# Two of the three conv projections of a two-layer mixer moved to matmuls with 512 moving columns, in two alternating bank pairs

## What is computed

```
proj = h @ w_in
b_a, c_a, x_a, u_p, q, k, v, ga, gp, gt = jnp.split(proj, split_points(), axis=-1)
y_a = short_conv_mixer(b_a, c_a, x_a, conv_w, w_a_out)

def short_conv_mixer(b_gate, c_gate, xin, conv_w, w_out):
    u = c_gate * xin
    y = lax.conv_general_dilated(u, conv_w, ..., feature_group_count=u.shape[-1])
    return (b_gate * y) @ w_out
```

## Time and profile before

| | us |
|---|---|
| median of 3 runs | 1310.85 (1310.82 to 1310.9) |
| the profiled execution | 1310.87 |
| its span, first to last instruction | 1309.1 |
| PE busy | 1293.9, 99% of the span |
| DVE busy | 1043.4, 80% |
| ACT busy | 715.8, 55% |
| PE in the 896 matmuls of L788 (narrow) | 112.2 |
| PE in the 1216 matmuls of L808 (wide) | 290.0 |

### The profile page before, as it was taken

How to read it: one execution, slowest core, us unless ns; L and a number is a source line. 1 busy time by engine, 2 the same in 40 slices (tenths; PEclk the granted TensorE clock), 3 DMA queues, 4 the chain that set the end, 5 groups by cost and what they waited for, 6 DMA issues and landing times.

```text
span 1309.1 us, 19856 instructions
## 1 busy us (share of the span) xinstructions
PE 1293.9 (99%) x7564; PEld 1122.8 (86%) x7564; DVE 1043.4 (80%) x1730; ACT 715.8 (55%) x1149; POOL 57.1 (4%) x108
## 2 busy tenths in 40 slices
PE   8999999999999999999999999999999999999998
PEld 7999898888888888998898888888879887888887
DVE  4887677877778786977687777788888898798888
ACT  5655655455454455555545464454477566655554
POOL 1111000000000000000000000000010000000000
PEclk9999999999999999999999999999999999999999
DMA  8865545764777745454446755878635515255551
GB/s 292 270 212 185 177 161 212 250 232 150 271 258 284 253 165 193 161 181 153 149 162 229 274 181 216 271 280 290 236 111 176 212 66 171 103 203 187 193 192 64
DMA packets 43000, 262.64 MB, mean 201 GB/s; under 512 B 5645, under 2 KB 6413, under 8 KB 15646
## 3 DMA queue, kind: packets, MB, share of 16 engines
q1 hardware_dynamic: 32688, 227.28, 48.9%
q0 software_dynamic: 10128, 34.06, 8.2%
q10 hardware_dynamic: 94, 0.07, 0.0%
HBM read 259.81 MB, written 1.58 MB: 200 GB/s over the span
## 4 chain that ended last, share of the span: by engine, by line
PE 94%; DVE 3%; ACT 1%; DMA 0%; issue 0%; SPq 0%; POOL 0%; DVEq 0%; POOLq 0%; ACTq 0%
PE psum L808 21%; PE psum L855 17%; PE psum L929 12%; PE psum L814 11%; PE psum L862 9%; PE psum L788 8%; PE psum L794 4%; PE psum L1017 1%; PE psum L1040 1%; PE psum L1203 1%; PE psum L1029 1%; PE psum L947 1%; DVE split L2164 1%; DMA ring<-stream 0%; PE psum L745 0%; PE psum L826 0%
## 5 line engine op out<-in xcount | busy, mean ns | idle before, releaser
L2164 DVE TENSOR_TENSOR split<-ring,split 128x1024 fp32r<-128x1024 f32 x406 | 479.3, 1219 | 59.7 <-ACT split L1571 58.4
L1571 ACT CAST split<-ring 128x1024 fp32r<-128x1024 f32 x405 | 405.7, 1050 | 174.8 <-PE psum L929 68.2
L808 PE MATMUL psum<-h,split 128*128 128x512 f32 x1216 | 290.0, 390 | 0.0
L808 PEld LDWEIGHTS psum<-h,split 128*128 128x128 f32 x1216 | 225.0, 188 | 44.7
L929 PE MATMUL psum<-split,feed 128*128 128x512 f32 x792 | 185.2, 390 | 0.0
L929 PEld LDWEIGHTS psum<-split,feed 128*128 128x128 f32 x792 | 146.8, 188 | 29.4 <-DVE split L2164 0.2
L814 PEld LDWEIGHTS psum<-h,split 128*128 128x128 f32 x1216 | 156.2, 191 | 6.1
L814 PE MATMUL psum<-h,split 128*128 128x256 f32 x1216 | 158.0, 283 | 0.0
L855 PE MATMUL psum<-split,h 128*128 128x512 f32 x632 | 155.8, 393 | 0.1
L855 PEld LDWEIGHTS psum<-split,h 128*128 128x128 f32 x632 | 116.3, 188 | 23.6 <-issue 0.4
L788 PE MATMUL psum<-h,split 128*128 128x256 f32 x896 | 112.2, 283 | 0.0
(11 more groups left out here) (378 smaller groups left out, 1365.0 us busy)
## 6 DMA issues: line engine op xcount, KB each, us to landing
ring<-stream SPq DMA_DIRECT2D x213, 1024.0 KB, 4.9
arena<-ada POOLq DMA_DIRECT2D x48, 512.0 KB, 5.8
arena<-bias_by_distance POOLq DMA_DIRECT2D x32, 96.0 KB, 5.2
gain<-norm_rows POOLq DMA_DIRECT2D x4, 512.0 KB, 6.0
x<-x_in SPq DMA_DIRECT2D x2, 512.0 KB, 4.1
ring<-stream SPq DMA_DIRECT2D x2, 512.0 KB, 6.9
arena<-norm_rows POOLq DMA_DIRECT2D x2, 512.0 KB, 5.7
gain<-mod_rows POOLq DMA_DIRECT2D x2, 512.0 KB, 6.0
```

The source lines that it names most:

```text
L808: pe.matmul(bank[b + m].rearrange("p (a t) -> p a t", a=2), w[0][:, k, m * P:(m + 1) * P], h[:, :, k, :], start=k == 0, stop=False)
L1571: act.copy(split_of(x)[:, 0, n], ring[:, AT[x] % RING, n]).then_inc(wh_ready, 1)
L2164: return dve.tensor_tensor(out_, value, high.bitcast(F32), ALU.subtract)
```

## The change

Job x and job b are done the wide way like c. The twelve conv jobs of a layer now take turns in two pairs of banks: 0 and 1 for c 0, 2 and 3 for x 0, 0 and 1 for b 0, 2 and 3 for c 1, and so on (`conv_bank`). PE therefore waits, ahead of each, until DVE has read the pair two jobs back (`wide_summed`). ACT has a copy of the cross part in x's slot, into `tmp`, and one in b's slot, into `stage` (signal `wide_cross`). DVE has an addition in each of these slots, and its multiplications then read SBUF alone.

```diff
--- before.py
+++ after.py
@@ -463,7 +463,8 @@
         yin_ready = sem("yin_ready")
         pooled_ready = sem("pooled_ready")
         feed_high = sem("feed_high")
-        c_summed = sem("c_summed")
+        wide_summed = sem("wide_summed")
+        wide_cross = sem("wide_cross")
         ao_split = sem("ao_split")
         ng_high = sem("ng_high")
         ng_ready = sem("ng_ready")
@@ -598,7 +599,11 @@
         def first_turned(kt):
             return bank[2 + kt][:, 0:T] if kt < 4 else bank[6 + kt % 2][:, (kt // 2 - 2) * T:(kt // 2 - 1) * T]
 
-        CONV_BANK = {"c": 0, "x": 2, "b": 3}
+        def summed(l, name, j):
+            return wide_summed, l * 12 + 3 * j + "cxb".index(name) + 1
+
+        def conv_bank(name, j):
+            return ({"c": 0, "x": 2, "b": 0}, {"c": 2, "x": 0, "b": 2})[j % 2][name]
 
         def q_bank(j):
             return (2, 0, 2, 4)[j]
@@ -1055,7 +1060,7 @@
                             pe.wait_ge(*release((name, j - 1), l))
                     elif name in ROW_JOBS:
                         if (name, j) == ("ga", 0):
-                            pe.wait_ge(c_summed, l * 4 + 4)
+                            pe.wait_ge(*summed(l, "x", 3))
                         elif j % 2 == 0:
                             pe.wait_ge(*release(LAYER_JOBS[k - 4], l))
                             pe.wait_ge(*release(LAYER_JOBS[k - 3], l))
@@ -1072,9 +1077,13 @@
                         if j == 0:
                             pe.wait_ge(q_sum_ready, l * 4 + 2)
                         else:
-                            pe.wait_ge(c_summed, l * 4 + j)
-                    elif name in ("x", "b"):
-                        pe.wait_ge(*release((name, j - 1) if j else ("kd", CONV_BANK[name] - 2), l))
+                            pe.wait_ge(*summed(l, "x", j - 1))
+                    elif (name, j) == ("x", 0):
+                        pe.wait_ge(*release(("kd", 1), l))
+                    elif name == "x":
+                        pe.wait_ge(*summed(l, "b", j - 1))
+                    elif name == "b":
+                        pe.wait_ge(*summed(l, "c", j))
                     elif k >= 4 and name != "wo" and LAYER_JOBS[k - 4][0] != "wo":
                         pe.wait_ge(*release(LAYER_JOBS[k - 4], l))
                     b = k % 4
@@ -1089,10 +1098,8 @@
                         mm = project_rows(c, h, k, (0, 1), {k_: (h_ready, k_ + 1) for k_ in range(KT)})
                     elif name == "q":
                         mm = project_both(q_bank(j), c)
-                    elif name == "c":
-                        mm = project_both(CONV_BANK[name], c)
-                    elif name in ("x", "b"):
-                        mm = project(CONV_BANK[name], c, h)
+                    elif name in ("c", "x", "b"):
+                        mm = project_both(conv_bank(name, j), c)
                     elif name == "wa":
                         if j == 0:
                             pe.wait_ge(yin_ready, l * 4 + 4)
@@ -1725,8 +1732,17 @@
                         act.copy(k_pair[:, 0, 2 * j:2 * j + 2, :], src).then_inc(kd_high, 1)
                     elif name == "c":
                         if j >= 1:
-                            act.wait_ge(dve_evac, l * len(DVE_JOBS) + dve_count(("x", j - 1)))
-                        act.copy(stage, cross_part(CONV_BANK[name])).then_inc(act_evac, 1)
+                            act.wait_ge(dve_evac, l * len(DVE_JOBS) + dve_count(("b", j - 1)))
+                        act.copy(stage, cross_part(conv_bank(name, j))).then_inc(act_evac, 1)
+                    elif name == "x":
+                        act.wait_ge(job_done, l * NJOBS + k + 1)
+                        if j >= 1:
+                            act.wait_ge(yin_ready, l * 4 + j)
+                        act.copy(tmp, cross_part(conv_bank(name, j))).then_inc(wide_cross, 1)
+                    elif name == "b":
+                        act.wait_ge(job_done, l * NJOBS + k + 1)
+                        act.wait_ge(dve_evac, l * len(DVE_JOBS) + dve_count(("x", j)))
+                        act.copy(stage, cross_part(conv_bank(name, j))).then_inc(wide_cross, 1)
                     elif name == "u":
                         act.copy(padded[:, :, PADW:PADW + T], src).then_inc(act_evac, 1)
                     if name == "wo" and j == 1:
@@ -2325,11 +2341,14 @@
                         link(dve.memset(upad, 0.0))
                     if name == "c":
                         dve.wait_ge(act_evac, l * len(ACT_JOBS) + act_count(("c", j)))
-                        dve.tensor_tensor(stage, main_part(CONV_BANK[name]), stage, ALU.add).then_inc(c_summed, 1)
+                        dve.tensor_tensor(stage, main_part(conv_bank(name, j)), stage, ALU.add).then_inc(wide_summed, 1)
                     if name == "x":
 
-                        dve.wait_ge(c_summed, l * 4 + j + 1)
-                        dve.tensor_tensor(upad[:, :, 1:1 + T], halves(CONV_BANK[name]), stage, ALU.mult).then_inc(dve_evac, 1)
+                        dve.wait_ge(*summed(l, "c", j))
+                        dve.wait_ge(wide_cross, l * 8 + 2 * j + 1)
+                        dve.tensor_tensor(tmp, main_part(conv_bank(name, j)), tmp, ALU.add).then_inc(wide_summed, 1)
+                        dve.wait_ge(*summed(l, "x", j))
+                        dve.tensor_tensor(upad[:, :, 1:1 + T], tmp, stage, ALU.mult).then_inc(dve_evac, 1)
                         dve.wait_ge(dve_evac, l * len(DVE_JOBS) + dve_count(("x", j)))
                         for tap in range(3):
                             for m in range(2):
@@ -2344,7 +2363,10 @@
                     elif name == "b":
                         if j >= 1:
                             dve.wait_ge(yin_ready, l * 4 + j)
-                        dve.tensor_tensor(tmp, halves(CONV_BANK[name]), y1, ALU.mult).then_inc(dve_evac, 1)
+                        dve.wait_ge(wide_cross, l * 8 + 2 * j + 2)
+                        dve.tensor_tensor(stage, main_part(conv_bank(name, j)), stage, ALU.add).then_inc(wide_summed, 1)
+                        dve.wait_ge(*summed(l, "b", j))
+                        dve.tensor_tensor(tmp, stage, y1, ALU.mult).then_inc(dve_evac, 1)
                         next_low((l, name, j))
                         dve.wait_ge(feed_high, l * 8 + j + 1)
                         low(feed[:, 1, pair], tmp, feed[:, 0, pair]).then_inc(yin_ready, 1)
```

## The result

| | us |
|---|---|
| median after, 4 runs | 1321.34 (1320.23 to 1321.44) |
| median before, 4 runs | 1310.88 (1310.82 to 1311.09) |
| ratio | 1.0078, 95% interval 1.0065 to 1.0090 |
| predicted | 1319.0, range 1316.5 to 1322.5 |

The change makes the kernel 10.5 us slower. The profiled execution took 1321.37 us with a span of 1319.6, which is 10.5 more than the span before. Three of the four executions had a mean granted clock of 0.996 or 0.997 and took 1321.32 to 1321.44 us; the fourth had 1.000 and took 1320.23 us. The profiled execution of the kernel before had 1.000.

A forecast was written before the change was run, and what follows sets the result against it. PE, busy for 99% of the span, was taken to bound the kernel. Waits of 11.01 us less savings of 2.88 gave +8.1: 1310.9 + 8.1 = 1319.0 us, range 1316.5 to 1322.5.

The forecast's parts named there:

- The saving: PE's x and b jobs in both layers: 16 fewer matmuls each, 0.18 us a job, 2.88 us less in all.
- the wait at x 0: Layer 0, PE at the start of x 0: waits 0.37 us until DVE has read both halves of the earlier bank pair.
- All seven places of the waits: PE at x 0 and after c 1, c 2, c 3 (layer 0); after c 1, c 2, ga 0 (layer 1): 11.01 us.
- The cycle of 20.3 to 20.4 us: DVE and ACT: products for x stand 20.3 to 20.4 us apart, against 18.55 for PE's own cycle.
- the 0.69 us assumed: DVE's product reading SBUF alone: put between 0.58 and 0.69 us, taken as 0.69 for the same engine and size.
- rival C: PE's clock falls to 1.2 GHz after a long wait, 3.8 us each: 1322.8 us after one, 1338 after five; chance 0.05.
- D: DVE's lag also delays weights' low parts and transposes; one more 1.8 us wait in each layer gives 1322.6 us; chance 0.07.
- the signals: Between engines, as from ACT's copy to DVE's addition: 0.04 us counted for each.
- the wait after c 1: Layer 0, PE ahead of the scores: waits 0.82 us for DVE's reading of the scores.
- The wait after c 2 in layer 0: PE ahead of the scores: waits 2.67 us for DVE's reading, with the scores at 90.61 and PE there at 87.94.
- A: Score readings still come in time everywhere, under 0.53 us of DVE delay in layer 1; only the saving stays: 1308.0 us; chance 0.05.
- B: Exponentials don't hold ACT's copy of x, DVE's idle time takes one addition a cycle, delay doesn't grow: 1313.1 us; chance 0.07.

The follow-up runs named there:

- the kernel without the added work: The change without ACT's copies and DVE's additions for x and b, cross parts left out of the result: 1308.67 us, ratio to before 0.9981.
- the two moves: The change with c slots' exponentials behind ACT's copy of x and b slots' scores read right behind b's product: 1308.58 us, ratio to before 0.9981.

## Why the prediction was right, point by point

*The saving.* 16 x 0.18 = 2.9, less the wait at x 0, was forecast for the matmuls alone and measured as 2.5 (the kernel without the added work). The Trainium skill, "TensorE: Matmul & The Clock Gate", section "Wait — 56ns, not 53.3ns?", states a fixed cost of about 2.5 ns a matmul; an estimate from it is 0.64 us for 256 fewer, and the measured 2.5 us disagrees with it.

*The additions and their place.* All seven places of the waits were forecast, and that none comes after c 3 in layer 1. The cycle of 20.3 to 20.4 us was met at 20.39. The product that reads SBUF alone, for which no row of before had a time, took the 0.69 us assumed. That the place of the work in the engines' orders makes the loss was an argument then, and the two moves show it: with every instruction of the change still there the time is 1308.6.

*What was mis-sized.* The forecast sum was +8.1 us, measured +10.5; the measured 1321.34 lies just above the 1317 to 1321 that the prediction called its own range, and inside the wider one only because that had room for the rivals C and D. First, the signals: I counted 0.04 us from ACT's copy to DVE's addition, and the trace has 0.12 to 0.14 (the copy of x 3 ends at 119.93 + 0.56 = 120.49, the addition starts at 120.62). Second, the first addition of layer 0 starts at 58.75, 0.55 after its copy ended (57.61 + 0.59 = 58.20), where 0.04 was counted; that makes the wait after c 1 1.31 instead of 0.82. It isn't so in layer 1 (0.14). Every run with a copy for x has a gap of 0.50 or 0.51 us there between DVE's memset (L2341) and the addition, and the two without that copy have none; what makes the gap is open. Third, the clock: rival C, with 0.05, came in a mild form. It was priced at 3.8 us for a fall that lasts a job; the falls last part of a pass and cost 1.1 net for both. With the 0.3 us by which the stretch starts later, that leaves 2.4 - 1.1 - 0.3 = 1.0 for the first two, of which 0.49 is the wait after c 1.

*What was luck.* The wait after c 2 in layer 0 was met to 0.02 us (2.69 for 2.67), but both of its ends came about 1 us later than forecast: the scores started at 91.58 for 90.61, and PE would have been free for them at 88.89 for 87.94. The measured waits come to 9.7 us for the forecast 11.0, so the sum of the waits was too high, and the slow clock, which the forecast left out of its sum, more than made up for it.

*The clock.* The Trainium skill, "TensorE: Matmul & The Clock Gate", section "HAM oscillation — how this bites in real kernels", has idle gaps of PE bring the clock down to half; no row of before showed it, and the trace of the change now does, with 0.50 behind waits of 2.1 us. What the prediction had wrong here is the chance: its rows ended at a wait of 1.6 us and said nothing on the longer ones that it forecast.

*The rivals.* A needed DVE to be less than 0.53 us late at the first meeting in layer 1, and it was 2.2 us late there (the reading ends at 551.59 + 0.08 = 551.67 instead of 543.70, and 5.79 of that is by how much job c 0 of this layer starts later, 525.50 for 519.71). B was priced at 1313.1 for a copy that the exponentials don't hold; with the exponentials of c's slots moved the time is 1315.8, more than that, because the copy stands ahead of the addition even so, with 0.76 us of idle time on DVE. B had that idle time take up the addition and the delay stop growing; it left out that the time goes to the copy, and DVE's cycle stays 0.78 us longer than PE's. Another 0.49 us is the wait after c 1. D did not happen: no wait of PE was released by a weight split in these stretches. The transposes that D also named did wait once, 0.59 us for ACT's copy.

## What to carry to other kernels

An engine that is busy for 99% of the span can still lose what an edit saves on it, if the edit lengthens the work ahead of a signal that it waits for: look up the slack of the tightest signal (here 0.53 us) before counting the saving. A hand-over through a second engine costs the time for which the receiver stands idle for it. That can be what stands ahead of it in the second engine's order (1.82 us behind the exponentials), its own duration and signal (0.76 us with the exponentials moved), or nothing where the receiver has other work meanwhile: the same matmuls, copy and addition cost 4.4 us in one job's slots and 0.8, not told from the noise, in another's. Where a signal is late, try first to move the instruction that gives the signal further up in its own engine's order, before removing work.

## What the hardware showed that was not expected

The granted clock fell from 2.4 to 1.2 GHz behind waits of 2.1 us (0.59 us of waiting and four transposes ahead of the first of them), twice in the profiled execution of the change and twice in that of its repeat, and did not behind waits of 1.3 and 1.7 us in the same one. Not every execution has it: one of the first four had a mean clock of 1.000. It lasted for part of one pass, which took 5.0 and 5.3 us instead of 3.7. Of the 3.2 us that this cost, the next waits gave back 2.1, since another engine set the pace.
